# A mixer's projections by seven products, and a sink as a score column: two edits of a two-block transformer kernel

## The chip, the cores and the metric

One core of a Trainium2 chip runs the whole program. The metric is the device time of one execution in microseconds (us). TensorE is called PE here, VectorE DVE, ScalarE ACT, GpSimd POOL, SyncE SP.

## The reference, cut to what matters

Two blocks of two layers run on x, 512 tokens by 1024 features, all in float32. The change touches two mixers of the second block:

```
def causal_depthwise_conv3(u, w):
    up = jnp.pad(u, ((0, 0), (CONV_W - 1, 0), (0, 0)))
    return up[:, 0:s] * w[0] + up[:, 1:s + 1] * w[1] + up[:, 2:s + 2] * w[2]

def short_conv_mixer(h, w_in, conv_w, w_out):          # w_in 1024 x 3072
    b_gate, c_gate, u = jnp.split(h @ w_in, 3, axis=-1)
    return (b_gate * causal_depthwise_conv3(c_gate * u, conv_w)) @ w_out

def sliding_window_sink_attention(q, k, v, sinks):
    # 16 heads of 64, 4 groups of 4 heads, 4 blocks of 128 tokens; each sees itself and the block before
    scores = jnp.where(valid, einsum(qb, kk) * scale, NEG)
    probs = softmax(concatenate([scores, sink], axis=-1))[..., :-1]
    return einsum(probs, vv)
```

Behind the convolution mixer stand its output product (1024 x 1024), a norm and a gated feed-forward net of width 2816 (gate and up in 22 tiles of 128, then down).

## The kernel before

**Products.** A float32 product is made of three fp32r matmuls, as each operand is split into a high part (fp32r) and a low part (what is left): `mm3` (L2174) issues high by high (L2176), high by low (L2178) and low by high (L2177). Activations lie as 8 depth tiles of 128 by 512 tokens (h_high, h_low). Weights come raw by DMA in chunks of 2048 columns a partition (`raw[0]`, `raw[1]`, in the rows w_raw), which SP starts as soon as their area is free; two neighbouring chunks are a pair. ACT makes the high part of a chunk in one instruction (`split_high`, L820), POOL the low part in eight pieces of 256 columns (`low`, L729; DVE takes some chunks).

**Order of the work.** Each engine runs its own program, and semaphores tie them. RING (L62) lists the stages with their pairs: ..., oout 4, cu 4, b 2, aout 2, gu0 11, dn0 6, kv, q, wo, gu1, dn1. cu and b are the projections of the convolution mixer, aout its output product, gu0 and gu1 the gate-and-up stages, dn0 and dn1 the down stages.

**cu and b.** `in_stage` (L2194) computes transposed tiles of 128 output features by 512 tokens, two tiles a chunk, in PSUM banks 0 to 3. A chunk of cu holds a tile of c and one of u; ACT copies the c tile to SBUF (gate_buf), DVE multiplies it by the u tile into conv_in (L1872), and convolves with one tensor_scalar and two scalar_tensor_tensor, each waiting for the one before:

```
v.tensor_tensor(cw[:, 2:], buf[s][:, :], PS[:, 2 * s + 1, :], ALU.mult).then_inc(pair_free[s], 1)
dve.wait_ge(pair_free[s], PF["cu"] + i + 1)
steps.link(v.tensor_scalar(cv[:, :], cw[:, 0:S], tap(0), None, ALU.mult))
steps.link(v.scalar_tensor_tensor(cv[:, :], cw[:, 1:1 + S], tap(1), cv[:, :], ALU.mult, ALU.add))
steps.link(v.scalar_tensor_tensor(yc[:, f, :], cw[:, 2:], tap(2), cv[:, :], ALU.mult, ALU.add))
```

A chunk of b holds two gate tiles, by which DVE multiplies the convolved ones (L1885); ACT makes the high part of the product (y_high, L1134), DVE its low part. Before each pair of cu chunks the last of the PE work of the norm ahead (transposes of x) is slotted in.

**A gate-and-up stage by seven products.** Its first two chunks are computed as above, the others (20) by a Strassen-Winograd scheme: a 1024 x 256 weight chunk and the tokens are cut into 2 x 2 blocks, and seven products of half size (depth 512, 128 columns, 256 tokens) take the place of eight. `seven_stage` (L2687) issues 7 x 4 x 3 matmuls of 256 columns. The seven weight operands ("slots") lie where the classical stages keep their split weights (`WH`, w_high). ACT makes their high parts (slot_high, L1185), POOL the low parts of slots 0, 2, 4 and 5 in 4 pieces each (L712), DVE those of 1, 3 and 6 (slot_low, L1964). DVE (`seven_dve`, L1927) also adds the weight blocks (sums at L1947, L1950, L1953, L1958, some in PSUM), combines products as they end (combinations at L1978, partial and joined; ACT copies one to SBUF first, first_copy, L1190, and adds or copies others, L1199), joins the last ones (L2002) and multiplies by the silu of the gate half (L2011). The sums of activation halves (h_sum_high, h_sum_low, first written to conv_sum areas) are made once, while the classical chunks run. The order of all of this is written out by hand around the index of the product.

**The banded attention.** A unit is a group of 4 heads and one of 4 token blocks, 16 in all. Per unit PE makes scores in PSUM, DVE masks them, scales and takes row maxima (L2116), takes the minimum with minus the sink (L2119) and the sink's exponent argument (L2121); ACT does the exponentials with row sums (L1291) and that of the sink (L1296); DVE adds the two sums (L2127), inverts (L2128) and multiplies (L2130, probs); PE transposes and multiplies by the values. Between units DVE and ACT turn the next group's queries by sines and cosines; the sine product is one instruction of 1024 columns from banks 0 and 1 (q_tmp, L2138).

## Time and profile before

| | |
|---|---|
| three runs | 1827.87, 1825.05, 1827.58 us (median 1827.58) |
| profiled execution | 1825.34 us, of which the span 1823.5 us |
| PE | 1768.3 us busy, 97%, 10272 matmuls |
| DVE | 1079.0 us, 59%, 1935 instructions |
| ACT | 799.7 us, 44%, 1325 |
| POOL | 794.1 us, 44%, 968 |
| granted PE clock | 9 tenths or more in each of the 40 slices |
| chain that ended last | PE 69%, issue 14%, POOL 7%, DVE 6%, ACT 3%, DMA 1% |
| HBM | 187.86 MB read, 104 GB/s over the span |

The profiled execution's own time is its span and 1.8 us around it. In the program's order the projections of the convolution mixer (cu and b) take 773.5 to 882.3 us, aout ends near 926, gu0 runs 954.4 to 1158.6, and the banded attention with its query product lies about 1318 to 1426. Busy shares average over stages with different limits; a row of a stage's own window tells what bounds it.

### The profile page before, as it was taken

The page shows a single profiled execution, that of the slowest core. Times are in us where ns is not written, and L with a number is a line of the kernel's source. Part 1 is how long each engine was busy: PE and PEld are TensorE (multiplying, and loading weights), DVE is VectorE, ACT ScalarE, POOL GpSimd, SP SyncE. Part 2 cuts the span into 40 slices and gives each one's busy share as a digit, 9 for nine tenths or more (in the row PEclk, how much of TensorE's full clock was granted, in tenths as well). Part 3 has the DMA queues.
Part 4 walks back from the last instruction along what each step waited for, and adds up shares of the span by engine and source line. Part 5 has one row for each costly group of instructions (what it writes and reads, how often), then busy time and mean ns, then how long its engine had stood idle before and what let it go on. Part 6 is the DMA issues. An engine that isn't in the chain of part 4 may idle for free.

```text
span 1823.5 us, 29057 instructions
## 1 busy us (share of the span) xinstructions
PE 1768.3 (97%) x10272; PEld 1533.2 (84%) x10272; DVE 1079.0 (59%) x1935; ACT 799.7 (44%) x1325; POOL 794.1 (44%) x968
## 2 busy tenths in 40 slices
PE   6999999989999999899999999999998999999998
PEld 5788888878887878888889999888965789999886
DVE  6774876476667654633187777412657388776312
ACT  3423331365655553422265555423556465555322
POOL 0365455440101061166466666463422176666461
PEclk9999999999999999999999999999999999999999
DMA  9543565321211233133323344322321123333321
GB/s 322 177 139 93 150 185 192 103 77 38 71 41 52 69 132 110 55 108 115 103 60 111 98 111 119 127 93 93 106 73 47 47 70 104 104 106 101 128 92 69
DMA packets 208788, 191.08 MB, mean 105 GB/s; under 512 B 10443, under 2 KB 188482, under 8 KB 208706
## 3 DMA queue, kind: packets, MB, share of 16 engines
q1 hardware_dynamic: 208064, 189.69, 33.4%
q8 instruction: 51, 0.84, 0.2%
q10 hardware_dynamic: 642, 0.29, 0.1%
q14 instruction: 31, 0.25, 0.0%
HBM read 187.86 MB, written 2.10 MB: 104 GB/s over the span
## 4 chain that ended last, share of the span: by engine, by line
PE 69%; issue 14%; POOL 7%; DVE 6%; ACT 3%; DMA 1%; SPq 0%; POOLq 0%; DVEq 0%; ACTq 0%
PE PS L2176 22%; PE PS L2177 22%; PE PS L2178 22%; POOL w_low L729 2%; POOL slot_low L712 2%; POOL w_low L743 1%; ACT w_high L820 1%; POOL a L696 1%; PE PS L2304 1%; DVE probs L2116 1%; DMA x<-in_x 1%; POOL w_low L753 1%; DMA w_raw<-in_o_w_out 0%; DVE ada_part L1356 0%; PE PS L2878 0%
## 5 line engine op out<-in xcount | busy, mean ns | idle before, releaser
L729 POOL TENSOR_TENSOR w_low<-w_raw,w_high 128x256 fp32r<-128x256 f32 x585 | 473.5, 845 | 633.7 <-ACT w_high L820 618.6
L820 ACT ACTIVATE w_high<-w_raw 128x2048 fp32r<-128x2048 f32 (+3 forms) x104 | 192.0, 1846 | 425.0 <-PE PS L2178 395.9
L2176 PE MATMUL PS<-h_high,w_high 128*128 128x512 f32 (+1 forms) x848 | 311.7, 368 | 9.3 <-DVE h_low L1641 2.4
L712 POOL TENSOR_TENSOR slot_low<-w_raw,slot_high 128x256 fp32r<-128x256 f32 x320 | 251.4, 812 | 144.2 <-ACT slot_high L1185 142.5
L2177 PE MATMUL PS<-h_low,w_high 128*128 128x512 f32 (+1 forms) x848 | 304.5, 359 | 0.0
L2178 PE MATMUL PS<-h_high,w_low 128*128 128x512 f32 (+1 forms) x848 | 304.3, 359 | 0.0
L2176 PEld LDWEIGHTS PS<-h_high,w_high 128*128 128x128 f32 x848 | 161.4, 190 | 38.8 <-issue 10.5
L2176 PE MATMUL PS<-h_sum_high,slot_high 128*128 128x256 f32 x640 | 181.5, 284 | 1.9 <-DVE joined L1978 1.3
L2178 PEld LDWEIGHTS PS<-h_high,w_low 128*128 128x128 f32 x848 | 161.3, 190 | 24.0
L2177 PE MATMUL PS<-h_sum_low,slot_high 128*128 128x256 f32 x640 | 181.1, 283 | 0.0
L2178 PE MATMUL PS<-h_sum_high,slot_low 128*128 128x256 f32 x640 | 181.1, 283 | 0.0
L2177 PEld LDWEIGHTS PS<-h_low,w_high 128*128 128x128 f32 x848 | 161.6, 191 | 20.4 <-issue 0.7
L2176 PE MATMUL PS<-h_high,slot_high 128*128 128x256 f32 x480 | 136.0, 283 | 1.3 <-ACT PS L1199 1.3
L2176 PE MATMUL PS<-w_high,ff_high 128*128 128x512 f32 x352 | 137.2, 390 | 0.0
L2178 PE MATMUL PS<-w_high,ff_low 128*128 128x512 f32 x352 | 137.0, 389 | 0.0
L2177 PE MATMUL PS<-w_low,ff_high 128*128 128x512 f32 x352 | 136.9, 389 | 0.0
L2177 PE MATMUL PS<-h_low,slot_high 128*128 128x256 f32 x480 | 135.8, 283 | 0.0
L2178 PE MATMUL PS<-h_high,slot_low 128*128 128x256 f32 x480 | 135.8, 283 | 0.0
L2176 PEld LDWEIGHTS PS<-h_sum_high,slot_high 128*128 128x128 f32 x640 | 122.8, 192 | 2.8 <-issue 1.8
L2178 PEld LDWEIGHTS PS<-h_sum_high,slot_low 128*128 128x128 f32 x640 | 122.8, 192 | 0.0
L2177 PEld LDWEIGHTS PS<-h_sum_low,slot_high 128*128 128x128 f32 x640 | 122.8, 192 | 0.0
L1185 ACT ACTIVATE slot_high<-w_raw 128x512 fp32r<-128x512 f32 x160 | 100.2, 627 | 46.0 <-PE PS L2178 43.4
(367 smaller groups left out, 3788.8 us busy)
## 6 DMA issues: line engine op xcount, KB each, us to landing
w_raw<-in_f_gate_up SPq DMA_DIRECT2D x88, 512.0 KB, 4.9
w_raw<-in_f_down SPq DMA_DIRECT2D x40, 512.0 KB, 4.2
w_raw<-in_e_w_in SPq DMA_DIRECT2D x32, 512.0 KB, 5.3
...
```

What stands on the lines that cost most here:

```text
L696: ins = nc.gpsimd.tensor_tensor(dst[:, b, j:j + 2, :], hH[of].bitcast(F32), hL[of].bitcast(F32), ALU.add)
L712: ins = nc.gpsimd.tensor_tensor(slotL[j][:, piece], src[:, piece], slotH[j][:, piece].bitcast(F32), ALU.subtract)
L729: ins = nc.gpsimd.tensor_tensor(WL[s][:, piece], raw[s][:, piece], WH[s][:, piece].bitcast(F32), ALU.subtract)
L743: ins = nc.gpsimd.tensor_tensor(WL[1][:, piece], raw[1][:, piece], WH[1][:, piece].bitcast(F32), ALU.subtract)
L753: nc.gpsimd.tensor_tensor(WL[1][:, h:], raw[1][:, h:], WH[1][:, h:].bitcast(F32), ALU.subtract).then_inc(pool_half, 1)
L820: nact(WH[s][:, 0:n], raw[s][:, 0:n], ACT.Copy).then_inc(w_high[s], 1)
L1185: nact(slotH[j][:, :], (b11, wsum2, t3, wsum1, b21, b22, wsum4)[j][:, :], ACT.Copy).then_inc(slot_high, 1)
L2116: ins = v.tensor_tensor_reduce(p2[n % 3][:, h, w:], raw_sc[:, h, w:], window[:, w:], 1.0, MASKED, ALU.add, ALU.max, st[:, 0, h:h + 1])
L2176: mm(dst, lh, rh, start=first, stop=False, skip_group_check=True)
L2177: mm(dst, lh, rl, start=False, stop=False, skip_group_check=True)
L2178: return mm(dst, ll, rh, start=False, stop=last, skip_group_check=True)
L2304: ins = tr(two(2 * t if b is None else b)[:, k, :], src[:, k * P:(k + 1) * P], ident)
```

## The change

**The convolution mixer.** cu and b become one stage, cub, of 6 pairs. The first two chunks stay classical (each a c tile and a u tile), the next six are conv chunks and the last four gate chunks, all ten by seven products with the code of the gate-and-up stages; the number of such chunks now depends on the stage, and ACT's and DVE's loops are unrolled there. ACT copies (no silu) what is multiplied. Per conv chunk DVE multiplies the joined u tile in PSUM by the c tile and convolves from PSUM: a tensor_scalar of 512 columns into y and two scalar_tensor_tensor that add 511 and 510 columns, each waiting for the one before (`convolve`). Per gate chunk it multiplies two tiles into y. y_high and y_low of the first six tiles of y are made while the last chunks run or behind them. Line numbers of cub's instructions in the changed kernel differ: slot_low L1941, combinations L1955, sums L1924, L1927, L1930 and L1935, join L1979, multiplication L1992.

**The next stage.** aout's two first high parts, which are 2048 columns wide where gu0's successor takes 1024, are now written by `seven_act` behind the last chunk's products, whose slots hold that area; its output order is 2, 0, 3, 1.

**The attention.** The score tile gets a 257th column that holds the sink (divided by the scale) for each head, so that the exponential's row sum contains it; L2121, L2127 and ACT's L1296 go, and a 128x4 tensor_scalar fills the column in the units with n % T < 2. Masked scores get two tiles of their own and probs two in place of three. The sine product is made in two halves of 512 columns, and PE waits for each bank's half where it waited for both.

```diff
-    ("cu", 4, (2, 2)),
-    ("b", 2, (2, 2)),
+    ("cub", 6, (2, 2)),
...
-N_SEVEN = F_TILES - 2
+N_SEVEN = {"cub": 10, "gu0": F_TILES - 2, "gu1": F_TILES - 2}
+CONV_CHUNKS = 6
...
-        p2 = [dz(f"probs2_{u}", o, [P, GROUP, 2 * P]) for u, o in enumerate((8576, 9600, 20864))]
+        masked2 = [dz(f"masked2_{u}", o, [P, GROUP, 2 * P + 1]) for u, o in enumerate((8576, 20864))]
+        p2 = [at(f"probs2_{u}", 192 * KB + 4128 * u, [P, GROUP, 2 * P + 1]) for u in range(2)]
...
+            with sp.Fori(4, 6) as i:
                 for s in range(2):
-                    load("b", i, s, cols(s, w_in["a_w_in"], i * 512 + s * 256))
+                    load("cub", i, s, two_tiles(s, w_in["a_w_in"], i * 512 + (s * 256 - 2048), i * 512 + (s * 256 + P - 2048)))
...
+                first_size = CHUNK if nxt == "aout" else D
+                gate = ACT.Copy if v.name == "cub" else ACT.Silu
...
-                        nact(WH[0][:, 0:D], raw[0][:, 0:D], ACT.Copy).then_inc(w_high[0], 1)
+                        nact(WH[0][:, 0:first_size], raw[0][:, 0:first_size], ACT.Copy).then_inc(w_high[0], 1)
...
+                if v.name == "cub":
+                    for i in range(1, last):
+                        pair(i)
+                    y_high(v, 0)
+                    y_high(v, 1)
+                    evacuate(last, 0, (last, 1))
+                    y_high(v, 2)
+                    y_high(v, 3)
+                    evacuate(last, 1, None)
+                    return
...
+            def y_high(v, f):
+                act.wait_ge(prod_ready, v.gated + (2 + CONV_CHUNKS + f // 2 + 1))
+                nact(yH[:, f, :], yc[:, f, :], ACT.Copy).then_inc(act_high, 1)
+
...
-                st, pr = soft[:, n % 2, :, :], p2[n % 3]
-                act.wait_ge(m2_ready, 2 * n + 1)
+                st = soft[:, n % 2, :, :]
+                act.wait_ge(m2_ready, n + 1)
                 for h in range(GROUP):
-                    nact(pr[:, h, w:], pr[:, h, w:], ACT.Exp, scale=SW_SCALE, bias=st[:, 2, h:h + 1], accum_out=st[:, 5, h:h + 1])
-                act.wait_ge(m2_ready, 2 * n + 2)
-                nact(st[:, 4, :], st[:, 3, :], ACT.Exp).then_inc(e2_ready, 1)
+                    ins = nact(p2[n % 2][:, h, w:], masked2[n % 2][:, h, w:], ACT.Exp, scale=SW_SCALE, bias=st[:, 2, h:h + 1], accum_out=st[:, 5, h:h + 1])
+                ins.then_inc(e2_ready, 1)
...
-                    v.tensor_tensor(cw[:, 2:], buf[s][:, :], PS[:, 2 * s + 1, :], ALU.mult).then_inc(pair_free[s], 1)
-                    dve.wait_ge(pair_free[s], PF["cu"] + i + 1)
-                    steps.link(v.tensor_scalar(cv[:, :], cw[:, 0:S], tap(0), None, ALU.mult))
-                    steps.link(v.scalar_tensor_tensor(cv[:, :], cw[:, 1:1 + S], tap(1), cv[:, :], ALU.mult, ALU.add))
-                    steps.link(v.scalar_tensor_tensor(yc[:, f, :], cw[:, 2:], tap(2), cv[:, :], ALU.mult, ALU.add))
...
-                        v.tensor_tensor(buf[m][:, :], PS[:, 2 * s + m, :], yc[:, f, :], ALU.mult).then_inc(prod_ready, 1)
...
                         slot_low(*following, 6)
                     dve.wait_ge(silu_ready, n * 2 + (v.silu + 4))
                     joins(4)
-                    f = i * 2 + s
-                    tt(ff[:, f, :], silu_out, joined[:, 0:2, :].rearrange("p a n -> p (a n)"), ALU.mult).then_inc(prod_ready, 1)
+                    other = joined[:, 0:2, :].rearrange("p a n -> p (a n)")
+                    if v.name != "cub":
+                        f = i * 2 + s
+                        tt(ff[:, f, :], silu_out, other, ALU.mult).then_inc(prod_ready, 1)
+                    elif n < CONV_CHUNKS:
+                        steps.link(tt(silu_out, silu_out, other, ALU.mult))
+                        convolve(silu_out, n + 2).then_inc(prod_ready, 1)
+                    else:
+                        f = (n - CONV_CHUNKS) * 2
+                        tt(yc[:, f, :], silu_out, yc[:, f, :], ALU.mult)
+                        tt(yc[:, f + 1, :], other, yc[:, f + 1, :], ALU.mult).then_inc(prod_ready, 1)
...
-                    nc.vector.tensor_tensor(ff[:, s, :], buf[s][:, :], PS[:, 2 * s + 1, :], ALU.mult).then_inc(prod_ready, 1)
+                    dst = cw[:, :] if v.name == "cub" else ff[:, s, :]
+                    nc.vector.tensor_tensor(dst, buf[s][:, :], PS[:, 2 * s + 1, :], ALU.mult).then_inc(prod_ready, 1)
+                    if v.name == "cub":
+                        dve.wait_ge(prod_ready, v.gated + s + 1)
+                        steps.link(convolve(cw[:, :], s))
...
+            def convolve(u, f):
+
+                def tap(j):
+                    return vec[:, f + (ROWS["conv"] + K * j):f + (ROWS["conv"] + K * j) + 1]
+
+                dst = yc[:, f, :]
+                steps.link(v.tensor_scalar(dst, u, tap(2), None, ALU.mult))
+                steps.link(v.scalar_tensor_tensor(dst[:, 1:], u[:, :S - 1], tap(1), dst[:, 1:], ALU.mult, ALU.add))
+                return v.scalar_tensor_tensor(dst[:, 2:], u[:, :S - 2], tap(0), dst[:, 2:], ALU.mult, ALU.add)
+
+            def y_low(f):
+                dve.wait_ge(act_high, LOWS["b"] + f + 1)
+                nc.vector.tensor_tensor(yL[:, f, :], yc[:, f, :], yH[:, f, :].bitcast(F32), ALU.subtract).then_inc(gate_low, 1)
...
+                sc = masked2[n % 2]
+                if n % T < 2:
+                    v.tensor_scalar(sc[:, :, 2 * P:].rearrange("p (o j) one -> p o (j one)", o=2), by_row(sinks[:, group]), 1.0 / SW_SCALE, None, ALU.mult)
                 dve.wait_ge(s2_done, n + 1)
-                if n >= 3:
-                    dve.wait_ge(t2_done, n - 2)
                 raw_sc = two(2).rearrange("p (h k) t -> p h (k t)", h=GROUP)
                 for h in range(GROUP):
-                    ins = v.tensor_tensor_reduce(p2[n % 3][:, h, w:], raw_sc[:, h, w:], window[:, w:], 1.0, MASKED, ALU.add, ALU.max, st[:, 0, h:h + 1])
+                    ins = v.tensor_tensor_reduce(sc[:, h, w:2 * P], raw_sc[:, h, w:], window[:, w:], 1.0, MASKED, ALU.add, ALU.max, st[:, 0, h:h + 1])
                 ins.then_inc(s2_read, 1)
                 dve.wait_ge(s2_read, n + 1)
-                v.scalar_tensor_tensor(pairs(2), pairs(0), -SW_SCALE, minus_sink, ALU.mult, ALU.min).then_inc(m2_ready, 1)
-                dve.wait_ge(m2_ready, 2 * n + 1)
-                v.tensor_tensor(pairs(3), sink, pairs(2), ALU.add).then_inc(m2_ready, 1)
...
-                steps.link(v.tensor_tensor(st[:, 6, :], st[:, 5, :], st[:, 4, :], ALU.add))
-                steps.link(v.reciprocal(st[:, 7, :], st[:, 6, :]))
-                pr = p2[n % 3][:, :, w:]
+                steps.link(v.reciprocal(st[:, 7, :], st[:, 5, :]))
+                pr = p2[n % 2][:, :, w:2 * P]
...
-                v.tensor_tensor(q2tmp[:, :, :], PS[:, 0:2, :], sin2, ALU.mult).then_inc(q2_sin, 1)
+                for m in range(2):
+                    v.tensor_tensor(q2tmp[:, m, :], PS[:, m, :], sinB, ALU.mult).then_inc(q2_sin, 1)
...
-            in_stage("cu", (TR["oout"], turn))
-            in_stage("b")
-            turn = turner("aout", 1, x_hat)
-            out_stage("aout", yH, yL, lambda kt: pe.wait_ge(gate_low, 2 + GATED["b"] + kt + 1), left("gu0"), turn=turn)
...
+            seven_stage(Seven("cub"), turn)
+            turn = turner("aout", 1, x_hat)
+            out_stage("aout", yH, yL, lambda kt: pe.wait_ge(gate_low, 2 + LOWS["b"] + kt + 1), gates_left(Seven("cub")), turn=turn,
+                      order=(2, 0, 3, 1))
...
-                    if g >= 2:
-                        pe.wait_ge(q2_sin, g - 1)
                 for j in range(first, last):
                     m, k = j // K, j % K
+                    if g >= 2 and k == 0 and tok.start == 0:
+                        pe.wait_ge(q2_sin, 2 * (g - 2) + m + 1)
```

DVE before, in the loop over cu (a chunk with a c and a u tile; register arithmetic left out, ISA rows are waits):

```order
L1872 TENSOR_TENSOR conv_in<-gate_buf_61,PS 128x512 [waits sg_ready]
L1874 ISA [waits pair_free0]
L1874 TENSOR_SCALAR conv_sum<-conv_in,vec 128x512
L1875 ISA [waits dve_step]
L1875 SCALAR_TENSOR_TENSOR conv_sum<-conv_in,vec,conv_sum 128x512
L1876 ISA [waits dve_step]
L1876 SCALAR_TENSOR_TENSOR conv_out<-conv_in,vec,conv_sum 128x512
L1872 TENSOR_TENSOR conv_in<-gate_buf_62,PS 128x512 [waits sg_ready]
```

In that loop nothing stands between one chunk's taps and the next chunk's multiplication.

DVE of the change, a conv chunk in the middle of the stage, from a combination to the next chunk's first (PS are PSUM banks, y is the convolved tile):

```order
L1955 TENSOR_TENSOR joined<-PS,partial_172 128x256 [waits seven_used,join_ready]
L1941 TENSOR_TENSOR slot_low_165<-PS,slot_high_158 128x512 [waits slot_high_ready]
L1924 TENSOR_TENSOR PS<-w_raw_50 128x512 [waits slot_dve,w_full1]
L1927 TENSOR_TENSOR PS<-w_raw_50,PS 128x512 [waits wsum_ready]
L1930 TENSOR_TENSOR w_raw_50<-w_raw_50 128x512 [waits wsum_ready]
L1979 TENSOR_TENSOR joined<-PS,partial 128x2x256 [waits seven_used]
L1941 TENSOR_TENSOR slot_low_168<-PS,slot_high_161 128x512 [waits slot_high_ready]
L1992 TENSOR_TENSOR PS<-PS,joined 128x512 [waits join_ready,silu_ready]
L2060 TENSOR_SCALAR y<-PS,vec 128x512 [waits dve_step]
L2061 SCALAR_TENSOR_TENSOR y<-PS,vec,y 128x511 [waits dve_step]
L2062 SCALAR_TENSOR_TENSOR y<-PS,vec,y 128x510 [waits dve_step]
L1955 TENSOR_TENSOR partial<-PS,first_copy 128x256 [waits seven_used,copy_ready]
```

The multiplication and the three taps, which followed each other in a loop, now stand between the join and the next chunk's first combination, and each waits for the one ahead.

DVE of the change at the stage's start, where the two classical chunks and the first seven-product chunk meet (L1913 and L1907 are low parts and sums of activation halves):

```order
L1913 TENSOR_TENSOR h_sum_low<-conv_sum_184,h_sum_high 128x1024 [waits hs_act]
L2004 TENSOR_TENSOR conv_in<-gate_buf_61,PS 128x512 [waits silu_ready]
L2060 TENSOR_SCALAR y<-conv_in,vec 128x512 [waits prod_ready]
L2061 SCALAR_TENSOR_TENSOR y<-conv_in,vec,y 128x511 [waits dve_step]
L2062 SCALAR_TENSOR_TENSOR y<-conv_in,vec,y 128x510 [waits dve_step]
L1941 TENSOR_TENSOR slot_low_163<-PS,slot_high_156 128x512 [waits slot_high_ready,dve_step]
L1913 TENSOR_TENSOR h_sum_low<-conv_sum_185,h_sum_high 128x1024 [waits hs_act]
L1907 TENSOR_TENSOR conv_sum_186<-conv_sum_a_181,conv_sum_184 128x1024 [waits hs_ready,half_sum]
L1941 TENSOR_TENSOR slot_low_165<-PS,slot_high_158 128x512 [waits slot_high_ready]
L1935 TENSOR_TENSOR PS<-w_raw_49,PS 128x512 [waits wsum_ready]
L2004 TENSOR_TENSOR conv_in<-gate_buf_62,PS 128x512 [waits silu_ready]
```

The first convolution stands ahead of the slots' low parts of the first chunk, and the second behind them.

ACT where aout's first weights are split, before (gate_buf holds products of b) and in the change:

```order
L1134 ACTIVATE y_high<-gate_buf_62 128x512
L820 ACTIVATE w_high_52<-w_raw_50 128x2048 [waits used1,w_full1]
L1134 ACTIVATE y_high<-gate_buf_61 128x512
L1134 ACTIVATE y_high<-gate_buf_62 128x512
L820 ACTIVATE w_high_51<-w_raw_49 128x2048 [waits used0,w_full0]
L820 ACTIVATE w_high_52<-w_raw_50 128x2048 [waits used1,w_full1]
```

```order
L1176 ACTIVATE first_copy<-PS 128x256 [waits seven_used]
L1182 ACTIVATE w_high_51<-w_raw_49 128x2048 [waits seven_used,w_full0]
L1185 ACTIVATE PS<-PS 128x256 [waits prod_ready,seven_used]
L1191 ACTIVATE w_high_52<-w_raw_50 128x2048 [waits seven_used,w_full1]
L1193 ACTIVATE PS<-joined 128x256 [waits join_ready]
L1246 ACTIVATE y_high<-y 128x512 [waits prod_ready] x2
L819 ACTIVATE w_high_51<-w_raw_49 128x2048 [waits used0,w_full0]
L1246 ACTIVATE y_high<-y 128x512 [waits prod_ready] x2
L819 ACTIVATE w_high_52<-w_raw_50 128x2048 [waits used1,w_full1]
```

The high parts of aout's first pair waited for the buffers of two finished chunks (used0, used1); now they wait for products of the last chunk (seven_used).

## Rows read from the trace of the kernel before

**Rows 1.** Windows: stretch us, length, busy PE, PEld, DVE, ACT, POOL, PEclk, DMA, GB/s.

```profile
773.50:882.30 108.80, 108.80 (x482) 90.12 (x481) 33.07 (x43) 25.65 (x23) 66.64 (x80) 1.00 0.35 108
954.40:1158.60 204.20, 202.55 (x1683) 201.81 (x1681) 150.42 (x243) 106.38 (x204) 126.18 (x162) 1.00 0.36 103
1318.00:1425.60 107.60, 98.21 (x581) 67.66 (x579) 68.87 (x223) 63.38 (x175) 26.26 (x32) 1.00 0.18 59
```

**Rows 2.** Timeline of PE at the mixer's end and in gu0: start, duration, engine, line.

```profile
882.11 0.39 PE L2178 MATMUL PS<-h_high,w_low 128*128 128x512 f32 x1
882.34 0.39 PE L2176 MATMUL PS<-w_high,y_high 128*128 128x512 f32 x1
...
970.00 0.28 PE L2177 MATMUL PS<-h_sum_low,slot_high 128*128 128x256 f32 x1
970.12 0.28 PE L2178 MATMUL PS<-h_sum_high,slot_low 128*128 128x256 f32 x1
```

**Rows 3.** Waits of PE in 940 to 1160, then in 1318 to 1426.

```profile
PE PS L2176 <- ACT PS L1199: 0.7, 1, 0.7
PE PS L2176 <- DVE joined L1978: 0.6, 1, 0.6
PE PS L2176 <- POOL slot_low L712: 0.3, 1, 0.3
...
PE PS L2866 <- DVE probs L2130: 6.2, 6, 2.1
PE PS L2176 <- DVE q_tmp L2138: 1.4, 3, 0.6
```

**Rows 4.** Lines' instructions: ns min/median/max, first and last start; and one of DVE's timeline.

```profile
L1874 DVE TENSOR_SCALAR conv_sum<-conv_in,vec x8: 486/486/490, 773.5 to 842.3; 128x512 f32<-128x512 f32 x8
L1875 DVE SCALAR_TENSOR_TENSOR conv_sum<-conv_in,vec,conv_sum x8: 750/998/1001, 774.2 to 843.0; 128x512 f32<-128x512 f32 x8
...
774.17 0.75 DVE L1875 SCALAR_TENSOR_TENSOR conv_sum<-conv_in,vec,conv_sum 128x512 f32<-128x512 f32 x1 [0.16 <-DVE conv_sum L1874]
...
L1679 DVE TENSOR_SCALAR latent_norm<-PS,stat x4: 482/483/484, 385.9 to 391.6; 128x256 f32<-128x256 f32 x4
```

**Rows 5.** Timeline of DVE at the start of gu0's seven products; idle before in brackets.

```profile
959.32 0.42 DVE L1978 TENSOR_TENSOR partial<-PS,first_copy 128x256 f32<-128x256 f32 x1 [2.33 <-ACT first_copy L1190]
...
967.86 0.69 DVE L1964 TENSOR_TENSOR slot_low<-PS,slot_high 128x512 fp32r<-128x512 f32 x1 [0.60 <-ACT slot_high L1185]
```

**Rows 6.** Windows ahead of the convolution mixer, columns as in Rows 1.

```profile
755.00:759.50 4.50, 1.09 (x8) 0.86 (x8) 2.26 (x2) 1.02 (x1) 0.00 (x0) 0.83 0.00 0
759.50:765.00 5.50, 5.32 (x25) 5.32 (x26) 0.12 (x1) 0.00 (x0) 0.00 (x0) 0.52 0.00 0
```

**Rows 7.** Timeline of DVE inside gu0, and the instructions of its sum at L1953.

```profile
971.87 0.68 DVE L1964 TENSOR_TENSOR slot_low<-PS,slot_high 128x512 fp32r<-128x512 f32 x1
972.47 0.41 DVE L1978 TENSOR_TENSOR partial<-PS,partial 128x256 f32<-128x256 f32 x1
972.80 0.68 DVE L1958 TENSOR_TENSOR PS<-w_raw,PS 128x512 f32<-128x512 f32 x1
...
L1953 DVE TENSOR_TENSOR w_raw<-w_raw x40: 682/834/1242, 948.2 to 1675.4; 128x512 f32<-128x512 f32 x40
```

**Rows 8.** Timelines of ACT and POOL behind gu0's last products, and during aout.

```profile
1154.54 1.06 ACT L1196 ACTIVATE w_high<-w_raw 128x1024 fp32r<-128x1024 f32 x1 [4.00 <-PE PS L2178]
...
1155.68 2.82 POOL L729 TENSOR_TENSOR w_low<-w_raw,w_high 128x256 fp32r<-128x256 f32 x4 [6.02 <-ACT w_high L1196]
...
893.48 1.92 ACT L820 ACTIVATE w_high<-w_raw 128x2048 fp32r<-128x2048 f32 x1 [7.92 <-PE PS L2178]
...
895.47 5.59 POOL L729 TENSOR_TENSOR w_low<-w_raw,w_high 128x256 fp32r<-128x256 f32 x8 [4.37 <-ACT w_high L820]
```

**Rows 9.** Timeline of DVE in one unit of the attention.

```profile
1409.01 0.16 DVE L2119 SCALAR_TENSOR_TENSOR soft<-soft,minus_sinks 128x4 f32<-128x4 f32 x1
...
1409.48 0.18 DVE L2128 RECIPROCAL soft<-soft 128x4 f32<-128x4 f32 x1
```

214 lines of the change are left out of this document (99 added, 115 removed).

## The prediction

> **What bounds the kernel now.** I read the windows first [rows 1]: in the convolution projections (773.5 to 882.3 us) TensorE (PE) is busy without a gap at clock 1.00, while VectorE (DVE) works 33.1 us of 108.8, ScalarE (ACT) 25.7 and GpSimd (POOL) 66.6. In the first gate-and-up stage, which already runs by seven products, PE is as full, and DVE works 150.4 of 204.2 us. The attention stretch leaves PE 9.4 us of 107.6 idle. So each matmul less pays in the first two, if the engines that prepare slots keep up, and waits pay in the third. Then the timelines of PE give the two rates: 128x512 matmuls start every 0.2267 us, 128x256 ones every 0.120 us [rows 2]. The waits by releaser show what PE waited for [rows 3].
>
> **The products.** A classical chunk is 2 tiles x 8 x 3 = 48 matmuls of 512 columns: 48 x 0.2267 = 10.88 us; from 773.5, ten chunks end at 882.3 as they should [rows 2]. A seven-product chunk is 7 x 4 x 3 = 84 matmuls of 256: 84 x 0.120 = 10.08. Both rates carry the same 13 ns above the columns' own time, and a seven-product chunk pays them 84 times instead of 48; so one eighth less work gives 7.4% less time. Ten chunks: **-8.0 us**. (The first two chunks stay classical, with the same half-token pieces.) The Trainium skill, page TensorE: Matmul & The Clock Gate, section Back-to-back issue gap, gives the step as N/2.4 ns plus about 2.5; by that a chunk would save 10.36 - 9.17 = 1.19 us and ten of them 11.9. The rows here show the larger fixed part, and the sum goes by the rows.
>
> **The start of the seven products.** The same code in the gate-and-up stage made PE wait three times, 0.7, 0.6 and 0.3 us, 1.6 together [rows 3]. In the convolution the DVE also has to run the taps: two classical chunks' worth and the first seven-product chunk's before PE has passed the second one's sixth product. A convolution is one tap of 0.49 and two of 0.75 to 1.00, each with 0.16 or more to the next, since it waits for the one before [rows 4]: about 2.8 us. Each multiplication ahead of it is now waited for too (0.69 + 0.16 in place of 0.60). Three of them add 3 x (2.8 + 0.25) = 9.1 us to a DVE queue which in the gate stage was full but for 2.33 + 0.60 us in this stretch [rows 5]. PE comes to the first product 2.2 us later than there, since 24 matmuls just before run at half clock (the clock rival has the working) [rows 6]. That leaves 9.1 - 2.9 - 2.2 = 4.0 us on top of the 1.6: 5.6, and 0.6 more because POOL's slot work stretches the two convolutions that read SBUF alone (1.00 against 0.75 [rows 4]): **+6.2 us**. Bounds: 1.6, where the order of the queue hides all three, and 9.5, where every tap is stretched.
>
> **The middle.** Per convolution chunk DVE now starts: three slot_low 0.60 each, three combinations 0.34, the join 0.60, four weight sums 0.73 + 0.61 + 0.60 + 0.60 [rows 7], the multiplication 0.84, and taps from PSUM. A first tap that reads PSUM is not in the trace at 512 columns: the SBUF form takes 0.49, the PSUM form at 256 columns 0.48 [rows 4], and 256 columns more cost 0.27 in slot_low against a combination [rows 7], so 0.75, the end nearer to its operands. With the waits: 0.91, 0.97 and 0.66. Together 9.4 us of 10.08: it fits, but the order matters. After a chunk's last product: join at +0.2, slot_low, multiplication at +1.5, taps until +4.9, combination 0.34, slot_low 0.60, combination 0.34, sum 0.60, combination 0.42 and 0.15 to PE: +7.35, and PE wants it at 5 x 1.44 = +7.2 for its sixth product. So 0.15 us in each of the five following chunks, **+0.8**; bounds 0 and 3.5. In the four gate chunks the taps are gone and one multiplication more (0.60) stands there: 0.
>
> **The turn to the next stage.** Behind the seven products of the gate stage ACT starts its 1024-column w_high at 1154.54 (1.06 us), and POOL's four pieces (2.82) end at 1158.50, when PE's last product ends too: no wait, but nothing to spare [rows 8]. For aout both are twice as long, 1.92 and 5.59 us [rows 8], and they can't start earlier, because the area is the slots of the last chunk. That is 0.86 + 2.77 = 3.6 us in which PE has no weights, where today the classical stage runs into aout with no wait (882.34 follows 882.11 by 0.23) [rows 2]. DVE works beside POOL then, and pieces can take longer, so **+3.8**; bounds 2.8 (ACT's part hidden) and 5.6 (all of POOL's). The order 2, 0, 3, 1 of the banks waits for gates that are long done by then.
>
> **The attention.** PE waits 6.2 us in six places for DVE's probs, before the transposes, and 1.4 in three for q_tmp [rows 3]. Per unit the change takes out DVE's L2121 and L2127 and ACT's L1296. From L2119 to L2128 it is 0.47 us now [rows 9]; without the two it is one issue, 0.08, so 0.39 less; 8 of 16 units get a 128x4 tensor_scalar (about 0.1) ahead of the scores. Where ACT ends last, 0.19 + 0.19 go instead. Each of the six waits shrinks by 0.4 to its end: **-2.4**, bounds 0 and -6.2. The sines are one instruction of 1024 columns today; a half of 512 is about 0.5 us shorter (twice the 0.27 of 256 columns [rows 7]), frees bank 0 that much earlier, and the m = 0 matmuls come first. The waits are 0.6 at most: **-1.3**, bounds -0.5 and -1.4. Two buffers for probs in place of three: ACT writes them only behind its own copy of the transposes, so no new wait.
>
> **Sum.** -8.0 + 6.2 + 0.8 + 3.8 = +2.8 in the convolution, -3.7 in the attention: -0.9 us. Against its own execution (1825.34, span 1823.5) that is 1824.4. The profiled one is near the low end of the three shown (median 1827.58); the mean of all four is 1826.5, so I write **1825.6 us**. A measurement of this kernel can tell about 0.2% (3.65 us) from no change, and this is less.
>
> **Rivals.**
> The convolution hides (chance 0.20). For it: DVE is idle 75 of 108.8 us in this stretch today [rows 1], and 9.4 of 10.08 fits. Then the start costs 1.6 as in the gate stage, the middle 0: -8.0 + 1.6 + 3.8 - 3.7 = -6.3, 1820.2 us from the same 1826.5. Against it: at the start the queue has no room [rows 5].
> VectorE becomes the bound (0.17, slower). Place: the taps of the convolution chunks. If those from PSUM are stretched beside POOL like the SBUF ones, 2 x 0.25 us a chunk come onto the path that stands at +7.35; from +7.2 on each tenth costs 0.5 us over five chunks. That is 2.5 more in the middle and 0.5 at the start; and the sum at L1953, 0.68 to 1.24 long [rows 7], would push the join by 0.3 in five chunks: 1.5 more. In all -0.9 + 4.5 = +3.6, 1830.1 us. Against it: slot_low, which reads PSUM, is 0.68 beside a busy POOL [rows 7].
> The clock falls (0.15). From 755.0 to 759.5 PE worked 1.09 us, and then ran at 0.52, the 1.2 GHz level: matmuls of 256 at 5.32 / 25 = 0.213 instead of 0.120, for 24 of them 2.2 us lost [rows 6]. A single wait of 2.1 us in the attention [rows 3] cost no clock: 1.00 there [rows 1]. The change makes one stall of 3.8 us ahead of aout and one near 2.7 in the second chunk. One fall: -0.9 + 2.2 = +1.3, 1827.8; two: +3.5, 1830.0. The Trainium skill, same page, section Why this matters for your kernels, warns of idle gaps between bursts of matmuls that bring the half clock back; by that rule the aout stall would do it, and the time be that of one fall.
> The attention change does nothing (0.08): the waits go over to the scores, or the third buffer was needed. +2.8, 1829.3 us.
> The forecast itself: 0.40.
>
> **Range and chances.** 1819.5 to 1831.5 holds the first rival at one end and VectorE as the bound at the other. Faster by over 0.2%: the first rival and a small part of the forecast's bounds, 0.25. Slower: most of VectorE's, a third of the clock's, a little of the last, 0.19. Within: 0.56.
>
> **What would show it.** Seven-product chunks start 10.08 us apart from the third on, 10.2 or so while the taps run. PE waits for DVE's conv_in product before the first chunk's third product (about 2 us), for joined twice (1 and 2.7), and once for POOL's w_low at aout (3.8). In the attention the probs waits fall from 6.2 to near 4 and q_tmp vanishes. I am wrong on the step if the start stalls are under 3 us or over 9, if chunks in the middle stand over 10.5 apart, if PEclk shows under 1.0 behind the aout stall, or if the probs waits stay at 6.

## The result

The changed kernel takes 1829.07 us (median of 20 runs, 1827.88 to 1830.12); the kernel before took 1826.30 us in 20 runs beside it (1824.92 to 1828.24). The ratio is 1.0015, 95% interval 1.0009 to 1.0021: slower by 2.8 us, where a small gain of 0.9 was forecast. The time lies in the stated range, but on the other side of no change.

The profiled execution of the changed kernel took 1829.39 us, span 1827.4; that of the kernel before 1825.34, span 1823.5. This pair is 3.9 us apart at the end of the span, since the profile of the kernel before lies 1 us under its median. The account below is made between the two profiles. The page's busy times of the changed kernel:

```profile
PE 1765.1 (97%) x10632; PEld 1547.0 (85%) x10632; DVE 1148.2 (63%) x2029; ACT 832.0 (46%) x1398; POOL 816.1 (45%) x988
```

PE is busy 3.2 us less and the span is 3.9 us longer: 7 us more are waits. Since a half-clock matmul counts as busy, the products saved more than 3.2 us.

**The mixer.** The timeline of PE in the changed kernel (start, duration, engine, line; in brackets the idle time before and its releaser): the first matmul of the second product in the fourth seven-product chunk, the same in the fifth, and then the last matmul of the last product and the first of aout:

```profile
814.89 0.28 PE L2192 MATMUL PS<-h_sum_high,slot_high 128*128 128x256 f32 x1
...
824.97 0.28 PE L2192 MATMUL PS<-h_sum_high,slot_high 128*128 128x256 f32 x1
...
883.89 0.28 PE L2194 MATMUL PS<-h_high,slot_low 128*128 128x256 f32 x1
...
887.54 0.50 PE L2192 MATMUL PS<-w_high,y_high 128*128 128x512 f32 x1 [3.38 <-POOL w_low L730]
```

A chunk takes 824.97 - 814.89 = 10.08 us, as forecast, taps or none. Up to 803 us, in the first two seven-product chunks, it is different. The waits of PE between 755 and 975 us (engine and line, waited for; us in total, times, longest), among which those for x_hat and h_low belong to the norm:

```profile
PE PS L2192 <- POOL w_low L730: 4.4, 2, 3.4
PE PS L2192 <- DVE joined L1955: 4.3, 3, 2.2
PE PS L2192 <- DVE h_low L1649: 2.4, 1, 2.4
PE PS L2318 <- DVE x_hat L1657: 2.1, 1, 2.1
PE PS L2192 <- ACT PS L1185: 1.2, 2, 0.7
PE PS L2192 <- DVE conv_in L2004: 1.1, 1, 1.1
```

(One wait for joined, 0.6, one of ACT's, 0.7, and the second for w_low, 1.1, stand in or ahead of gu0. The first two are as in [rows 3], and the last took 0.8 in the kernel before.) And windows of the same kernel (columns as in Rows 1):

```profile
773.50:800.00 26.50, 21.12 (x170) 20.37 (x169) 25.16 (x38) 11.28 (x22) 15.67 (x20) 1.00 0.29 80
800.00:825.00 25.00, 25.00 (x199) 25.00 (x198) 21.49 (x36) 12.13 (x23) 14.71 (x19) 0.93 0.32 85
825.00:850.00 25.00, 25.00 (x211) 25.00 (x210) 22.92 (x40) 12.99 (x25) 14.97 (x21) 1.00 0.44 121
```

```profile
887.50:930.00 42.50, 42.45 (x180) 34.99 (x181) 17.42 (x18) 12.48 (x19) 14.12 (x16) 0.96 0.33 100
```

DVE works 25.16 of the first 26.5 us: here its queue is the bound. In the window from 800 us PE's clock is down to 0.93, in the one from 887.5 us to 0.96: matmuls of 256 columns follow each other by 0.213 us instead of 0.120 from 800.01 to 803.21, and those of 512 by 0.43 instead of 0.227 from 888.92 to 891.91.

**Ahead of the mixer** stands what I had not looked at. DVE's timeline in the norm, in the kernel before and in the changed one, each followed by its PE row for the transposes of the third token tile; the last row is POOL's in the changed kernel:

```profile
740.99 1.28 DVE L1636 SCALAR_TENSOR_TENSOR x<-x,mv,gains 128x1024 f32<-128x1024 f32 x1
742.31 1.28 DVE L1637 SCALAR_TENSOR_TENSOR x<-x,stat,gains 128x1024 f32<-128x1024 f32 x1
743.51 2.28 DVE L1366 TENSOR_TENSOR w_low<-w_raw,w_high 128x2048 fp32r<-128x2048 f32 x1
747.20 1.22 DVE L1619 SCALAR_TENSOR_TENSOR x<-x,hf 128x1024 f32<-128x1024 f32 x1
...
750.22 1.03 PE L2304 MATMUL PS<-small,x_hat 128*128 128x128 f32 x8
```

```profile
741.29 1.82 DVE L1644 SCALAR_TENSOR_TENSOR x<-x,mv,gains 128x1024 f32<-128x1024 f32 x1
743.15 1.64 DVE L1645 SCALAR_TENSOR_TENSOR x<-x,stat,gains 128x1024 f32<-128x1024 f32 x1
744.71 2.83 DVE L1374 TENSOR_TENSOR w_low<-w_raw,w_high 128x2048 fp32r<-128x2048 f32 x1
748.95 1.67 DVE L1627 SCALAR_TENSOR_TENSOR x<-x,hf 128x1024 f32<-128x1024 f32 x1
...
752.33 1.09 PE L2318 MATMUL PS<-small,x_hat 128*128 128x128 f32 x8 [1.60 <-DVE x_hat L1657]
...
740.59 10.60 POOL L697 TENSOR_TENSOR conv_sum_a<-h_high,h_low 128x256 f32<-128x256 f32 x8 [0.80 <-DVE h_low L1649]
```

These four instructions are the same in both kernels. They take 1.90 us longer in the second, because POOL, idle there before, now makes the sums of activation halves that the seven products need, from the moment two token tiles are ready. PE waits 1.6 us for x_hat and starts the stage 2.3 us later (762.26 against 759.68 is 2.6, of which 0.3 is older than this stretch).

**The attention** answers [rows 3]; its waits in 1318 to 1430 us of the changed kernel:

```profile
PE PS L2883 <- DVE probs L2145: 4.3, 5, 1.6
...
PE PS L2192 <- DVE q_tmp L2154: 0.5, 1, 0.5
```

### The profile page after: what moved, and what is told of

It is laid out like the page before. It is cut to its first block, busy times and chain, and to the rows that moved or that the text cites. A ratio compares the mean times of both kernels' runs of the same rounds, so it can differ in the third digit from the quotient of the medians.

```text
span 1827.4 us, 30058 instructions
## 1 busy us (share of the span) xinstructions
PE 1765.1 (97%) x10632; PEld 1547.0 (85%) x10632; DVE 1148.2 (63%) x2029; ACT 832.0 (46%) x1398; POOL 816.1 (45%) x988
## 4 chain that ended last, share of the span: by engine, by line
PE 67%; issue 14%; POOL 7%; DVE 7%; ACT 3%; DMA 1%; SPq 0%; POOLq 0%; DVEq 0%; ACTq 0%
PE PS L2192 21%; PE PS L2194 21%; PE PS L2193 21%; POOL w_low L730 2%; POOL slot_low L713 2%; POOL w_low L744 1%; ACT w_high L819 1%; POOL gate_sum_a L697 1%; PE PS L2318 1%; DVE ada_part L1364 1%; DVE masked L2134 1%; POOL w_low L754 1%; DMA ada_raw<-in_ada_w 1%; DMA w_raw<-in_o_w_out 0%; PE PS L2895 0%
## 5 line engine op out<-in xcount | busy, mean ns | idle before, releaser
L730 POOL TENSOR_TENSOR w_low<-w_raw,w_high 128x256 fp32r<-128x256 f32 x513 | 415.6, 844 | 560.8 <-ACT w_high L819 538.7
L713 POOL TENSOR_TENSOR slot_low<-w_raw,slot_high 128x256 fp32r<-128x256 f32 x400 | 315.3, 814 | 183.8 <-ACT slot_high L1171 181.4
L2192 PE MATMUL PS<-h_high,w_high 128*128 128x512 f32 (+1 forms) x688 | 249.5, 363 | 8.9 <-POOL w_low L730 2.5
L2193 PE MATMUL PS<-h_low,w_high 128*128 128x512 f32 (+1 forms) x688 | 241.8, 351 | 0.0
L2194 PE MATMUL PS<-h_high,w_low 128*128 128x512 f32 (+1 forms) x688 | 241.7, 351 | 0.0
L2192 PE MATMUL PS<-h_sum_high,slot_high 128*128 128x256 f32 x800 | 227.1, 284 | 6.6 <-DVE joined L1955 5.0
L2194 PE MATMUL PS<-h_sum_high,slot_low 128*128 128x256 f32 x800 | 226.6, 283 | 0.0
L2193 PE MATMUL PS<-h_sum_low,slot_high 128*128 128x256 f32 x800 | 226.6, 283 | 0.0
L2192 PE MATMUL PS<-h_high,slot_high 128*128 128x256 f32 x600 | 170.6, 284 | 1.9 <-ACT PS L1185 1.9
L1171 ACT ACTIVATE slot_high<-PS 128x512 fp32r<-128x512 f32 x150 | 89.4, 596 | 110.1 <-PE PS L2194 96.7
```

Of the source, the lines that this page charges most:

```text
L713: ins = nc.gpsimd.tensor_tensor(slotL[j][:, piece], src[:, piece], slotH[j][:, piece].bitcast(F32), ALU.subtract)
L730: ins = nc.gpsimd.tensor_tensor(WL[s][:, piece], raw[s][:, piece], WH[s][:, piece].bitcast(F32), ALU.subtract)
L1171: nact(slotH[j][:, :], (b11, wsum2, t3, wsum1, b21, b22, wsum4)[j][:, :], ACT.Copy).then_inc(slot_high, 1)
L2192: mm(dst, lh, rh, start=first, stop=False, skip_group_check=True)
L2193: mm(dst, lh, rl, start=False, stop=False, skip_group_check=True)
L2194: return mm(dst, ll, rh, start=False, stop=last, skip_group_check=True)
```

## The account between the two profiles

| term | forecast | found, by starts of PE's matmuls |
|---|---|---|
| offset from the program's first stages | none | +0.3 |
| norm ahead of the mixer, stretched by POOL | none | +2.3 |
| products, ten chunks | -8.0 | -8.0 (ten of 10.08 for ten of 10.88) |
| waits in the first two seven-product chunks | +6.2 | +6.3 (1.2, 1.7, 0.7, 2.4, and 0.3 for the slow matmul behind each) |
| middle of the stage | +0.8 | 0.0 |
| half clock in the first chunks | rival | +1.5 (15 matmuls at 0.213 us) |
| fewer half-clock matmuls ahead of them (15, not 22) | none | -0.7 |
| turn to aout | +3.8 | +3.5 |
| half clock behind it | rival | +1.8 (42.55 for 40.80 us) |
| attention | -3.7 | -3.2 |
| sum | -0.9 | +3.8 |

## The experiments

Twelve kernels, each with five rounds against the kernel before; the change stands at 1.0015 on this scale. Theory: the parts are independent, and the loss sits in the norm (POOL), in the start (DVE's queue), at aout (POOL's low part), and in half-clock stretches behind two of these.

**1. The attention alone** (the kernel before with these hunks of the change):

```diff
-                sc = p2[n % 3][:, :, w:]
+                sc = masked2[n % 2]
...
-                v.tensor_tensor(pairs(3), sink, pairs(2), ALU.add).then_inc(m2_ready, 1)
...
-                v.tensor_tensor(q2tmp[:, :, :], PS[:, 0:2, :], sin2, ALU.mult).then_inc(q2_sin, 1)
+                for m in range(2):
+                    v.tensor_tensor(q2tmp[:, m, :], PS[:, m, :], sinB, ALU.mult).then_inc(q2_sin, 1)
```

> The kernel before with the attention's part of the change alone (sink as a score column, sine product in halves). The trace of the changed kernel shows PE's waits in the attention 3.2 us shorter than before. Theory A, the two parts are independent: -3.2 us against the kernel before (ratio 0.9983), waits for probs near 4.3 and for q_tmp near 0.5 us in the attention's stretch. Rival B, the gain in the attention stood there only because the stretch came later or otherwise phased in the whole change: within 1 us of the kernel before.

Measured: 1822.73 us, ratio 0.9982 (0.9973 to 0.9991), -3.2 us. PE waits 4.3 us for probs and 0.5 for q_tmp, the figures of the whole change.

**2. The convolution alone** (the change with those hunks taken back).

```diff
+                sc = p2[n % 3][:, :, w:]
-                sc = masked2[n % 2]
...
```

> The changed kernel with the attention of the kernel before: the convolution mixer's part of the change alone. Theory A (independent parts): +6.0 us against the kernel before (the change's +2.8 without the attention's -3.2; ratio 1.0033), with the same three places as in the changed kernel: two DVE stretches in the norm ahead 2.2 us longer, 6.0 us of waits in the first two seven-product chunks, 3.5 us ahead of aout, and two stretches of PE at half clock behind them. Rival B: under +4 us, if part of the loss came from the attention's new buffers.

Measured: 1833.17 us, ratio 1.0038 (1.0024 to 1.0052), +7.2 us. The same waits stand in the same places (1.60 for x_hat, 1.05, 1.50, 0.58 and 2.21 in the first chunks, 3.38 ahead of aout) and both half-clock stretches. With the first run: -3.2 + 7.2 = +4.0, which the intervals of the two allow beside the change's +2.8. Within these intervals the parts are independent, and the convolution is a loss by itself.

**3. POOL's half sums one token tile later.**

```diff
-                pool.wait_ge(h_ready, T * v.q + 2)
+                pool.wait_ge(h_ready, T * v.q + (3 if v.name == "cub" else 2))
```

> The changed kernel, but POOL's sums of activation halves for the convolution mixer start one token tile later (they wait for the third tile's h_low, not the second's). Theory A: they stretched DVE's norm instructions that read SBUF alone (1.28 us each before, 1.82 and 1.64 beside POOL) and so made PE's 1.6 us wait for x_hat at 750.5; with POOL silent there each takes 1.28 again, that wait goes, the first products of the stage start 2 us earlier, and the time is 1.5 to 2 us below the changed kernel's (about +1 us against the kernel before, ratio 1.0005). Rival B, the stretching is not POOL's: nothing changes there, and the sums come later, so the second half-sum on DVE waits: 0 to +3 us against the changed kernel. Rival C: the norm is faster, but the same 2 us come back as longer waits in the first two seven-product chunks, since DVE's queue there is what ends last: within 0.5 us of the changed kernel.

Measured: 1826.08 us, ratio 1.0002 (0.9993 to 1.0011), so 2.4 us off the change. The same rows of DVE's timeline, and POOL's:

```profile
741.63 1.28 DVE L1644 SCALAR_TENSOR_TENSOR x<-x,mv,gains 128x1024 f32<-128x1024 f32 x1
742.95 1.28 DVE L1645 SCALAR_TENSOR_TENSOR x<-x,stat,gains 128x1024 f32<-128x1024 f32 x1
744.16 2.29 DVE L1374 TENSOR_TENSOR w_low<-w_raw,w_high 128x2048 fp32r<-128x2048 f32 x1
...
754.99 6.50 POOL L697 TENSOR_TENSOR conv_sum_a<-h_high,h_low 128x256 f32<-128x256 f32 x8 [14.87 <-DVE h_low L1649]
```

Back to 1.28 and 2.29, and the wait for x_hat of 1.60 is gone. POOL's own eight pieces take 6.50 us in place of 10.60. By the starts of PE's matmuls the norm gives back 2.3 us (the stage starts at 760.32, against 762.26, and this profile began the stretch 0.3 later). Two more things differ between these two profiles: the classical chunks ahead take 1.0 us more (24 half-clock matmuls, not 15), and the second seven-product chunk takes 12.60 us for 14.11, since behind its 2.2 us wait there is no half clock this time. The Trainium skill, page SBUF — State Buffer, section SBUF: two separate sides, says that VectorE and GpSimd share one pair of ports, which one instruction holds whole while the other waits, and counts VectorE's operations with two inputs in SBUF among those concerned. The trace agrees: both engines lengthen (1.28 to 1.82, 6.50 to 10.60), and VectorE's operations that read PSUM don't, below.

**4. aout's first low part on DVE** (and POOL begins with the second chunk):

```diff
+                if name == "aout":
+                    first = 1
+                    low(0, 1)
...
+                    if v.name == "cub" and not following:
+                        split_low("aout", 0, 0)
                     product(7)
```

> The changed kernel, but the low part of aout's first chunk is made by DVE in one instruction of 2048 columns (2.3 us in the trace, ended by 884.2) in place of POOL's eight pieces (5.55 us, ended at 887.5). Theory A: the 3.4 us wait ahead of aout falls to 0.3 or less, and since PE then doesn't stand still, it doesn't fall to half clock behind it either (1.7 us): -5 us against the changed kernel, -2.2 against the kernel before (ratio 0.9988). Rival B: the half clock comes all the same (it follows from something else): -3.3. Rival C: the next wait, for DVE's join and the product of the last gate chunk, takes its place: -1 to -2, with a wait for y_low or prod in the second or third bank.

Measured: 1823.57 us, ratio 0.9987 (0.9978 to 0.9996), 5.1 us off the change. DVE's instruction, and aout's window:

```profile
881.48 2.29 DVE L1377 TENSOR_TENSOR w_low<-w_raw,w_high 128x2048 fp32r<-128x2048 f32 x1 [1.51 <-ACT w_high L1185]
```

```profile
883.80:926.40 42.60, 42.57 (x195) 35.48 (x196) 19.34 (x20) 16.30 (x23) 16.35 (x19) 1.00 0.33 100
```

2.29 us on DVE for what takes POOL 5.55 in the changed kernel; DVE stood idle for 3.82 us in that place. No wait ahead of aout is left (3.3 us less from the last matmul to aout's first), and the clock behind it is 1.00 (aout's stretch takes 40.9 us, not 42.55): the half clock there follows from PE's standing still.

**5. Two taps left out in the classical chunks** (the first two feature tiles of the output lack them).

```diff
-                        steps.link(convolve(cw[:, :], s))
+                        steps.link(nc.vector.tensor_scalar(yc[:, s, :], cw[:, :], vec[:, s + ROWS["conv"]:s + ROWS["conv"] + 1], None, ALU.mult))
```

> The changed kernel without the two scalar_tensor_tensor of the convolution in each of the two classical chunks (four instructions of 1.11 us and their waits; the output's first two feature tiles then lack two of three taps; nothing else is left out). It measures what these taps cost at the start of the stage. Theory A, DVE's queue there is what ends last, and every microsecond taken from it ahead of the second seven-product chunk comes off PE's waits until those of the gate-and-up stage are left (1.6 us): the waits of 6.0 us fall to 1.6 to 2, and with them the half clock behind the last: -4 to -5.5 us against the changed kernel, ratio to the kernel before 0.9985 to 0.9993. Rival B, POOL's slot work or ACT's copies end just behind DVE there: the waits stay over 3.5 us with POOL's slot_low or ACT's slot_high as releaser, -2 us at most.

Measured: 1826.74 us, ratio 1.0005 (0.9996 to 1.0014), 1.8 us off the change and less than expected. The waits (745 to 930 us):

```profile
PE PS L2192 <- DVE joined L1955: 3.1, 2, 2.2
...
PE PS L2192 <- ACT PS L1185: 0.6, 1, 0.6
```

The one for conv_in is gone, and the first for joined fell from 1.50 to 0.85; the one of 2.2 us stayed (2.21). Theory A was too simple: the start is not one queue from end to end. DVE catches up in PE's first waits, and the long one, in the second chunk, has its own cause. (This profile is the fastest of the run's eleven executions, 1.8 us under their median, and has no half clock in the first chunks; others may have it.)

**6. The taps moved to ACT and POOL.** ACT scales by each tap, POOL adds:

```diff
+                    for j, dst in enumerate((yc[:, f, :], cw[:, :], yc[:, K - 1 - f, :])):
+                        nact(dst, yc[:, K - 1 - f, :], ACT.Copy, scale=tap).then_inc(z_dve, 1)
...
+                    nc.gpsimd.tensor_tensor(yc[:, f, d:], yc[:, f, d:], src[:, :S - d], ALU.add).then_inc(z_pool, 1)
```

> The changed kernel, whole, with the convolution of the two classical chunks moved off DVE: ACT scales by the three taps (six instructions of 512 columns) and POOL adds (four) while the first three seven-product chunks run. Theory A: as in the run with two taps left out, or 0.3 us better, since all three taps are gone from DVE's queue: -4 to -5.8 us against the changed kernel, ratio to the kernel before 0.9983 to 0.9993. Rival B: ACT's six copies (some 0.6 us each) or POOL's additions (some 1.5 us each) delay slots of the second to fourth chunk: new waits for slot_high or slot_low of 1 to 4 us, and the time stays within 1.5 us of the changed kernel's.

Measured: 1834.81 us, ratio 1.0050 (1.0036 to 1.0064). The reason is a wait I put in myself. POOL's timeline and the waits:

```profile
804.38 1.26 POOL L724 TENSOR_TENSOR y<-y,conv_in 128x511 f32<-128x511 f32 x1 [13.06 <-ACT conv_in L1250]
```

```profile
PE PS L2222 <- POOL slot_low L713: 5.2, 1, 5.2
```

POOL works one chunk ahead of ACT, so its addition, placed behind its second chunk, stood for 13 us in front of the third chunk's slots, until ACT's copies came. PE waited 5.2 us and ran 36 matmuls at half clock around that. Two of the additions are seen here at 1.26 and 1.09 us.

**7. Cures 3 and 4 together** (both diffs above).

> Both cures at once: POOL's half sums one token tile later, and aout's first low part on DVE. Alone they gave ratios of 1.0002 and 0.9987 where the change has 1.0015, so -2.4 and -5.1 us. Theory A, they are at different places and add: -7.5 us against the changed kernel, ratio 0.9974 (0.9966 to 0.9982). Rival B: what is won in the norm is given back in the first chunks once both are in: ratio 0.9987.

Measured: 1821.54 us, ratio 0.9978 (0.9968 to 0.9987): they add, and the kernel is by the ratio 4.0 us faster than the kernel before, though its profile has the half clock of the first chunks (from 799.03).

**8. Both, and the taps as in run 6.**

> All three: half sums later, aout's first low part on DVE, and the classical chunks' taps on ACT and POOL. Theory A, additive: the 7.5 us of the two and 4 to 5 of the taps, -12 us against the changed kernel, ratio to the kernel before 0.9950 (0.9940 to 0.9960), no wait over 1 us between the first classical chunk and aout. Rival B: with the half sums later and the taps gone, the sums of activation halves (POOL's second, then DVE's) are what the third product waits for: a wait of 1 to 3 us there, ratio 0.9960 to 0.9970.

Measured: 1827.27 us, ratio 1.0005 (0.9996 to 1.0014). The expected 0.9950 is missed by 10 us. Additivity is not tested by this, since the 5.17 us wait of run 6 is in it.

**9. The weight sums moved.** In the first chunk DVE's order behind the last product is: join, low parts, multiplication, three taps, and three weight sums of the next-but-one chunk; only then the second chunk's combinations. Here the sums go behind the second chunk's third combination, and the low parts of the next chunk's slots, which need them, behind the sums:

```diff
+                        if second:
+                            sums(*following, (1, 2, 3))
+                            slot_low(*following, 1)
+                            sums(*following, (4,))
...
-                    if begin:
+                    if begin and v.name != "cub":
                         sums(*after, (1, 2, 3))
```

> The changed kernel with one thing moved: at the first seven-product chunk DVE made the next-but-one chunk's first three weight sums (2.1 us) behind that chunk's convolution and ahead of the second chunk's combinations; here they come behind the second chunk's third combination. The run with two taps left out took 2.3 us off the changed kernel (ratio 1.0005 to 1.0015), but left the wait of 2.2 us before the second chunk's sixth product untouched, so the taps of the classical chunks are not its cause. Theory A: its cause is DVE's queue right ahead of the combinations, convolution (2.3) and sums (2.1) in a row: the wait goes (0 to 0.3 left), and -2.2 us, or -3.5 with the half clock that follows it in some executions; ratio to the kernel before 0.9996 to 1.0004. Rival B: the sums, now later, are what ACT's slot_high and the slots of the third chunk wait for: the wait comes back 5 to 10 us later with 1 to 2 us, and ratio 1.0008 to 1.0015.

Measured: 1828.87 us, ratio 1.0013 (1.0004 to 1.0022). The waits (745 to 930 us):

```profile
PE PS L2196 <- DVE joined L1955: 2.7, 2, 1.5
...
PE PS L2196 <- DVE joined L1983: 1.3, 1, 1.3
```

The 2.2 us wait at the second chunk's sixth product is gone, and 1.28 and 1.20 came up in the next chunk, in its third and sixth product. Rival B: the backlog moves on, it doesn't vanish.

**10. The first conv chunk's taps cut** (one multiplication in place of three taps, so the third feature tile of the output is not the convolution):

```diff
-                        convolve(silu_out, n + 2).then_inc(prod_ready, 1)
+                        if n:
+                            convolve(silu_out, n + 2).then_inc(prod_ready, 1)
+                        else:
+                            tt(yc[:, 2, :], silu_out, other, ALU.mult).then_inc(prod_ready, 1)
```

> The changed kernel with the three taps of the first seven-product chunk replaced by one multiplication (its feature tile of the output is not the convolution; all else whole). Theory A (queue of convolution and sums ahead of the second chunk's combinations): 1.6 us less on DVE there, and the 2.2 us wait falls to 0.6; -1.6 us or, without the half clock, up to -3; ratio 1.0000 to 1.0008. Rival B: the wait is set by POOL's or ACT's slots: it stays at 2.2 us and the ratio at 1.0015.

Measured: 1828.99 us, ratio 1.0014 (1.0005 to 1.0023). The wait fell from 2.22 to 0.95, much as theory A says, but one of 0.74 came in the chunk after, and the time didn't move beyond its interval. What is taken from DVE at one point of the start was worth half or less of itself in runs 5 and 10. The reading that PE, no longer waiting, asks for the next thing sooner fits the waits that came up later in runs 9 and 10; it was not tested by itself.

**11. Cures 3, 4 and 9.**

> Half sums later, aout's first low part on DVE, and the weight sums moved: the whole change is computed. Theory A: the 7.1 us of the first two (ratio 0.9978) and the 2.2 of the third add: ratio 0.9966 (0.9958 to 0.9974), some 1819.5 to 1821 us. Rival B: with the half sums later the start is tighter and the third gives nothing: 0.9978.

Measured: 1821.80 us, ratio 0.9975 (0.9965 to 0.9984): within its interval of run 7; moving the sums gives nothing measurable here.

**12. The same, with the taps on ACT and POOL,** ACT's first three copies now one chunk earlier than in run 6 and POOL's additions one chunk later:

```diff
-                            if i == 1 and s == 1:
-                                tap_sum(0, 1)
...
+                            if i == 2:
+                                tap_sum(0, s + 1)
...
-                        if i == 1:
-                            scaled(0)
+                        if i in (1, 2):
+                            scaled(i - 1)
```

> The same, and the classical chunks' taps on ACT and POOL, now with POOL's additions one chunk later than in the run that stood at 1.0050: there POOL waited 5.2 us for ACT's scaled copies, because it works one chunk ahead of ACT. Theory A: with POOL behind ACT nothing waits, and the waits before the third product of the first chunk (1.1) and before its sixth (1.5) fall to 0.4 together: another -2.2 us, ratio 0.9954 (0.9946 to 0.9962). Rival B: ACT's or POOL's extra work (3.6 and 6 us in two chunks' time) delays a slot by 1 to 3 us: ratio 0.9962 to 0.9975.

Measured: 1818.39 us, ratio 0.9958 (0.9945 to 0.9972): 7.7 us faster than the kernel before and, by the two ratios, 10.4 faster than the change. Its waits (745 to 930 us) in the mixer and at aout:

```profile
PE PS L2228 <- DVE joined L1986: 1.6, 2, 1.2
PE PS L2228 <- DVE joined L2016: 1.3, 1, 1.3
PE PS L2228 <- POOL w_low L747: 0.8, 1, 0.8
PE PS L2228 <- ACT PS L1205: 0.2, 1, 0.2
```

and its windows over the stage:

```profile
773.00:800.00 27.00, 25.18 (x206) 24.61 (x205) 23.26 (x37) 15.37 (x31) 18.13 (x22) 1.00 0.29 79
800.00:825.00 25.00, 23.81 (x199) 23.63 (x198) 23.47 (x39) 13.90 (x26) 18.99 (x24) 1.00 0.46 127
```

Against the changed kernel's rows of the same stretches: PE is busy 25.2 us of 27 where it was 21.1 of 26.5, with the clock at 1.00 in both; and in the next 25 us there are waits where the changed kernel had the half clock (1.00 for 0.93). Backlog is left in the third chunk (1.28 and 1.19). Whether the taps' cure is better without run 9's move wasn't tried.

## Why the prediction was wrong

**Products, -8.0:** right to the tenth, with 10.08 us a chunk from the third on.

**The start, +6.2:** 6.3 found. The places were right: a wait for conv_in (forecast 2, found 1.1) and two for joined (1 and 2.7; 1.5 and 2.2), and one for ACT (0.6), which the list of signs didn't have. That three convolutions feed them is shown by runs 5 and 10, each of which shrinks the waits just behind the taps that it cuts. What was wrong is the arithmetic that treats microseconds put into the queue, or taken from it, as microseconds of time: run 5 took four instructions of 1.11 us out and won 1.8. The sum also counted 24 half-clock matmuls ahead, where 15 came. So its hitting 6.3 is in part luck.

**The middle, +0.8:** found 0. DVE's timeline in the third seven-product chunk, which starts at 803.39, from the multiplication to the next combination:

```profile
804.83 0.69 DVE L1992 TENSOR_TENSOR PS<-PS,joined 128x512 f32<-128x512 f32 x1
805.55 0.75 DVE L2060 TENSOR_SCALAR y<-PS,vec 128x512 f32<-128x512 f32 x1
...
807.79 0.41 DVE L1955 TENSOR_TENSOR partial<-PS,first_copy 128x256 f32<-128x256 f32 x1
```

From start to start that is 2.96 us, where 3.38 were summed: an instruction that waits for the one ahead starts 0.03 to 0.04 us behind its end, not 0.16. So the last combination ends 6.7 us into the chunk, not 7.2, in time for the sixth product. VectorE as the bound fails on its first condition, that taps from PSUM lengthen beside POOL. All lines with instructions of the taps in the changed kernel:

```profile
L2061 DVE SCALAR_TENSOR_TENSOR y<-PS,vec,y x6: 749/750/751, 793.0 to 846.6; 128x511 f32<-128x511 f32 x6
L2061 DVE SCALAR_TENSOR_TENSOR y<-conv_in,vec,y x2: 1108/1111/1114, 772.4 to 780.0; 128x511 f32<-128x511 f32 x2
```

From PSUM 750 ns six times out of six, with POOL busy or not; from SBUF 1111.

**The turn, +3.8:** 3.5 found, ACT's 1.92 and POOL's 5.55 as in [rows 8]. ACT starts at 879.95, when the fourth product ends, as worked out.

**The attention, -3.7:** 3.2 found and measured alone. (The rival in which it does nothing gives +2.8, the measured figure, and is wrong all the same: run 1 excludes it.) The waits for probs fell by 1.9 (forecast 2.4), those for q_tmp by 0.9 (1.3); the rest is smaller waits that shifted.

**The step that failed** is the claim, never written out, that nothing ahead of 773.5 us changes. Every instruction that the change issues was added up for DVE, and not for POOL: its eight additions of activation halves are in no term of the sum. They are hidden by themselves, since POOL was idle there, but they made others longer. The price stood in the rows: 0.75 against 1.00 [rows 4] was applied to two taps (0.6 us), and not to the norm, whose DVE chain feeds x_hat and so PE: 2.3 us, and the same 2.3 come back in run 3's profile. That alone turns -0.9 into a loss.

**The clock** was named as a rival at 0.15, and it happened. Its price was 2.2 us a fall, and found were 1.5 and 1.8. The rival's time for two falls, +3.5, is near the profiles' +3.9, but by luck: it has too much for the clock and nothing for the norm. Behind aout the fall should have been in the forecast itself. The row against it, a 2.1 us wait at clock 1.00, speaks of waits of 2 us; the forecast stall was 3.8. Every profile with the 3.4 us stall (the change and runs 2, 3, 5, 6, 9, 10) shows half clock behind it, and the five without it (4, 7, 8, 11, 12) don't. The Trainium skill, page TensorE: Matmul & The Clock Gate, section Why this matters for your kernels, warns of idle gaps between bursts of matmuls, since they bring the half clock back; behind this stall the trace agrees, with 0.96 in aout's window. The fall in the first chunks is less sure: behind the same 2.2 us wait the changed kernel and runs 2 and 7 show it, as do 6 and 8 behind 2.06 us, and runs 3, 4 and 5 don't.

With these two the forecast would have been -0.9 + 2.3 + 1.8, and 1.5 more where the first fall comes: +3.2 to +4.7 before the fewer slow matmuls (-0.7), against the 2.8 measured and 3.9 between the profiles.
